# Three passes instead of triples: the order of the split products in a chunk, and where TensorE waits for the low weights

## The chip, the core and the metric

The kernel runs on one core of a Trainium2 chip. Its engines work side by side and meet through semaphores: TensorE (PE) multiplies, VectorE (DVE), ScalarE (ACT) and GpSimd (POOL) do the elementwise work, SyncE (SP) issues loads. The metric is the device time in microseconds of one execution; the median over several executions counts.

## What is computed

The reference is one inference step of a decoder trunk of two layers, for 256 prompt positions and 8 sampled ones (264 token columns in all), with a model width of 2048. Cut to what matters here:

```python
def _layer(x, ...):
    xn = _rms_norm(x, g_pre_mix)
    proj = xn @ w_in                       # 2048 x 6144 columns here
    ...                                    # retention, mLSTM and pooling heads on proj
    mixed = concatenate([ret_out, mlstm_out, pool_out]) @ w_out
    x = x + _rms_norm(mixed, g_post_mix)
    hn = _rms_norm(x, g_pre_ffn)
    ff = (silu(hn @ w_ffn_gate) * (hn @ w_ffn_up)) @ w_ffn_down
    x = x + _rms_norm(ff, g_post_ffn)
```

All of it is in fp32. The outputs are the updated x for prompt and samples and the new states of the heads, for both layers. Nearly all arithmetic lies in the four matrix products with `w_in`, `w_out`, gate and up, and down.

## The kernel before, in words

Activations lie transposed, with 128 features on the partitions and the 264 tokens as columns. A weight matrix comes in **chunks**: a chunk is 128 x 2048 words and holds sixteen 128 x 128 blocks of weights, all that one output tile of 128 features needs (for the down projection a chunk has eleven blocks, and an output tile takes two chunks). A layer has 216 chunks, numbered in the order of their use: 0 to 47 for `w_in`, 48 to 63 for `w_out`, 64 to 107 gate and up of the first half of the hidden units, 108 to 139 down for it, 140 to 183 and 184 to 215 the same for the second half.

An fp32 product is done as three products in a faster rounded format (fp32r). Each operand is split into a rounded high part and a low part, the rest. A block's product is then high weights x high operand, high weights x low operand, low weights x high operand, all added up in one PSUM bank. These are lines 463, 464 and 465, three matrix products of 128 x 128 weights by 264 columns for each block, 48 in a chunk.

A chunk passes through four engines:
- SP loads it into one of four slots of `raw` (line 395) when the chunk four before it has been used.
- ACT copies it, rounded, into one of two slots of `whi` (line 741, the high part), when it has landed and the chunk two before it has been used. It counts `hi_made`.
- DVE subtracts high from raw and writes the low part `wlo` over the raw slot (line 1010). It counts `chunk_split`.
- TensorE waits for a free PSUM bank (`tile_evac`) and for `chunk_split`, does the 48 products, and counts `chunk_used`.

DVE then takes the result out of the bank. In the projections of `w_in` it multiplies it by the reciprocal norm (lines 1278 to 1291); the four banks 0 to 3 are used in turn.

The order of the work on each engine is written out by hand. Between the chunks of `w_in` a table, `SCHEDULE`, puts steps of the heads on every engine: TensorE does chunk n and then its part of the steps listed for n, DVE and ACT their parts of the same steps and their part of the split for chunk n + 2. For n from 15 to 41 DVE does the steps first and the low part of chunk n + 2 behind them (line 1300). Retention head h has its scores behind chunk 29 + 2h (`ret_scores`, L618), its states behind chunk 30 + 2h (`ret_states`, L626 and L630) and its outputs behind chunk 31 + 2h (`ret_outputs`, L640 to L645). The outputs wait for DVE's lines 1197 and 1203 (`ret_s2`, `ret_snew`).

Two kinds of chunks are special. The first chunk after a norm (0 and 64, `fresh`) has the sums of squares for the norm between its products (`square_sum`, L439) and waits for each block of its operand. Chunk 48, the first of `w_out`, does the block of the last retention head at its end and waits for it there (`last_ready`); its start also waits for the pooling heads (`pl_lo`).

Of the kernel before, what the change touches and what calls it, by code (L numbers as in the profile page):

```python
# [23 lines left out]
P = 128  # L24
# [3 lines left out]
KT = D_MODEL // P  # L28
# [162 lines left out]
def build(nc, a, gamma, gchunk):  # L191
    with ExitStack() as ctx:
# [3 lines left out]
        start = base0 - 212800  # L196

        def place(name, shape, dt, at=None):

            n = 4  # L200
            for s in shape[1:]:
                n *= s
            if at is None:
                at = used[0]
                used[0] += (n + 31) // 32 * 32
                assert used[0] <= 212800, (name, used[0])
            t = nc.alloc_sbuf_tensor_at(name, shape, dt, offset=start + at)
            return t, at
# [11 lines left out]
        wlo, _ = place("wlo", [P, RAW, CHUNK], F32R, at_raw)  # L220
# [69 lines left out]
        late = proj[:, T_MO:NPROJ, :].rearrange("p a t -> p (a t)")  # L290
# [18 lines left out]
        def cnt(name, unit=1, head=0):  # L309
            c = Count(sem(name), unit, head)  # L310
            if head:
                ahead.append(c)
            return c
# [5 lines left out]
        hi_made = cnt("hi_made")  # L319
        chunk_split = cnt("chunk_split")  # L320
# [101 lines left out]
        def _(pe):  # L422
            pe.wait_ge(*dve_done(3))
            with pe.Fori(0, DEPTH) as l:
# [11 lines left out]
                def square_sum(m, k):  # L436

                    pe.wait_ge(*sqx_made(l * 2 * KT + m * KT + k + 1))
                    pe.matmul(bank[4][:, 0:TOK], ones, sq[:, k % 4, :], start=k == 0, stop=k == KT - 1)\  # L439
                        .then_inc(*sqx_used.up)  # L440

                def chunk(n, slot, hi_slot, out, operand, ks, start, stop, fresh=None, last_ready=None):

                    if fresh:
                        e, m, lead = fresh
                        pe.wait_ge(*rms_made(l * 4 + e))
                        for k in range(lead):
                            square_sum(m, k)  # L450
                    pe.wait_ge(*chunk_split(n + 1))
                    high = whi_spare if hi_slot is None else whi[:, hi_slot]
                    for k, tile in enumerate(ks):
                        w = bass.ds((tile - min(ks)) * P, P)
                        hi, lo = operand(tile)
                        first, last = start and k == 0, stop and k == len(ks) - 1
                        if last and last_ready:
                            pe.wait_ge(*last_ready)
                        if fresh:
                            if k + lead < KT:  # L460
                                square_sum(m, k + lead)
                            pe.wait_ge(*operand_lo(l * 2 * KT + m * KT + k + 1))
                        pe.matmul(out, high[:, w], hi, start=first, stop=False)  # L463
                        pe.matmul(out, high[:, w], lo, start=False, stop=False)  # L464
                        mm = pe.matmul(out, wlo[:, slot, w], hi, start=False, stop=last)  # L465
                    mm.then_inc(*chunk_used.up)


# [9 lines left out]
                def whole_tile(c, o, j, operand, fresh=None, hi_slot=0):  # L478

                    pe.wait_ge(*tile_evac(o - BANKS + 1))  # L480
                    chunk(c, j, hi_slot, bank[j][:, 0:TOK], operand, range(KT), True, True, fresh)
# [207 lines left out]
                for j in range(RAW):  # L689
                    c, o_ = l * N_CHUNKS + C_OUT + j, l * N_TILES + O_OUT + j  # L690
                    if j == 0:

                        pe.wait_ge(*tile_evac(o_ - BANKS + 1))
                        pe.wait_ge(*mixed_ready(2 * l + 1))
                        pe.wait_ge(*pl_lo(l + 1))
                        chunk(c, j, 0, bank[j][:, 0:TOK], of_mixers, [k for k in range(KT) if k != RH - 1] + [RH - 1],
                              True, True, last_ready=mixed_ready(2 * l + 2))
                    else:
                        whole_tile(c, o_, j, of_mixers, hi_slot=j % HI)
                whole(1, KT // RAW, C_OUT, O_OUT, of_mixers)  # L700
                acc_sum(1)
                for b in range(NBLK):
                    if b == 0:
                        for j in range(RAW):
                            whole_tile(l * N_CHUNKS + C_GU[0] + j, l * N_TILES + O_GU[0] + j, j, of_x,
                                       (2, 1, 2) if j == 0 else None, FIRST_GU[j])
                    whole(1 if b == 0 else 0, 2 * BT // RAW, C_GU[b], O_GU[b], of_x)
                    with pe.Fori(0, KT // 4) as i:
                        for j in range(8):
                            u, half = j // 2, j % 2  # L710
                            if j < 2:
                                pe.wait_ge(*hidden_ready(l * FT + b * BT + (half + 1) * HT))
                            if half == 0:
                                pe.wait_ge(*tile_evac(l * N_TILES + O_DN[b] + i * 4 + u - BANKS + 1))
                            chunk(l * N_CHUNKS + C_DN[b] + i * 8 + j, j % RAW, j % HI, bank[u][:, 0:TOK], of_hidden,
                                  range(half * HT, (half + 1) * HT), half == 0, half == 1)
# [926 lines left out]
```

## Time and profile before

| | |
|---|---|
| median of 3 runs | 2576.87 us (2573.36 to 2578.7) |
| the profiled execution | 2579.15 us |
| its span (first to last instruction) | 2577.5 us |
| PE busy | 2496.9 us, 97% |
| PE weight loads busy | 2454.4 us, 95% |
| DVE busy | 1438.3 us, 56% |
| ACT busy | 1060.9 us, 41% |
| POOL busy | 301.8 us, 12% |
| mean granted TensorE clock | 0.984 of full |
| chain of work that ended last | PE 90% of it; L463, L464 and L465 28% each |

Busy times are those of one execution. Matrix products are pipelined: each is shown for about 0.28 us, but one starts about every 0.12 us, so a busy share near 100% says that the stream does not break, and how fast it runs is read from start to start. An engine's idle time matters only where the next engine waits for it. The view of who waited for whom takes an idle time from the modelled end of the instruction before.

### The profile page before, as it was taken

What the parts mean: (1) busy time and instruction counts of PE and PEld (TensorE: products, weight loads), DVE (VectorE), ACT (ScalarE), POOL (GpSimd) and SP (SyncE); (2) the same over time, 40 slices, a digit from 0 to 9 for tenths busy, and PEclk for the clock granted to TensorE, in tenths of its full rate; (3) what the DMA queues carried; (4) which work ended last, traced back from release to release, by engine and by line L of the source; (5) the groups of instructions that cost most, each with busy time, mean ns of one, the idle gap of its engine ahead of it and who ended that gap; (6) DMA issues with size and microseconds to landing.
All of it is one profiled execution on the core that took longest, in us unless ns stands there. A gap on an engine that the chain in (4) does not pass through costs nothing.

```text
span 2577.5 us, 50784 instructions
## 1 busy us (share of the span) xinstructions
PE 2496.9 (97%) x20192; PEld 2454.4 (95%) x20192; DVE 1438.3 (56%) x1669; ACT 1060.9 (41%) x1298; POOL 301.8 (12%) x264
## 2 busy tenths in 40 slices
PE   8999999899999999999899999998999999999996
PEld 7999999899999999999799999898999999999996
DVE  5577564755554455554575774647555544555445
ACT  5433554444433343333344345534443333343432
POOL 1001143400000000002310012343000000000023
PEclk9999999999999999999899999999999999999998
DMA  6444644355545555545444455443555455555453
GB/s 256 166 164 141 209 158 171 123 180 179 180 164 181 195 182 184 183 162 181 167 161 172 150 163 190 148 176 118 181 180 182 166 179 194 184 182 181 158 182 118
DMA packets 70613, 443.86 MB, mean 172 GB/s; under 512 B 8512, under 2 KB 8736, under 8 KB 31456
## 3 DMA queue, kind: packets, MB, share of 16 engines
q1 hardware_dynamic: 62784, 413.23, 45.9%
q0 software_dynamic: 6992, 26.82, 3.3%
q10 hardware_dynamic: 720, 2.24, 0.2%
q8 instruction: 74, 1.21, 0.2%
q14 instruction: 43, 0.35, 0.0%
HBM read 427.10 MB, written 15.16 MB: 172 GB/s over the span
## 4 chain that ended last, share of the span: by engine, by line
PE 90%; DVE 3%; issue 3%; ACT 2%; POOL 1%; DMA 1%; DVEq 0%; ACTq 0%; POOLq 0%; SPq 0%
PE bank L463 28%; PE bank L464 28%; PE bank L465 28%; DVE wlo L1010 1%; ACT whi L741 1%; PE bank L574 1%; PE bank L645 1%; POOL x L1421 1%; PE bank L439 1%; PE bank L492 1%; DMA pool_p<-proj 0%; DVE alo L1016 0%; DVE work L1027 0%; PE bank L529 0%; ACT v_spread L851 0%
## 5 line engine op out<-in xcount | busy, mean ns | idle before, releaser
L463 PE MATMUL bank<-ahi,whi 128*128 128x264 f32 x4288 | 1231.4, 287 | 8.4 <-DVE wlo L1010 6.8
L465 PE MATMUL bank<-ahi,wlo 128*128 128x264 f32 x4352 | 1236.1, 284 | 0.0
L464 PE MATMUL bank<-alo,whi 128*128 128x264 f32 x4288 | 1218.8, 284 | 0.0
L741 ACT ACTIVATE whi<-raw 128x2048 fp32r<-128x2048 f32 (+1 forms) x428 | 751.7, 1756 | 1124.6 <-PE bank L465 1117.1
L1010 DVE TENSOR_TENSOR wlo<-raw,whi 128x2048 fp32r<-128x2048 f32 (+1 forms) x428 | 897.5, 2097 | 561.3 <-ACT whi L741 561.1
L463 PEld LDWEIGHTS bank<-ahi,whi 128*128 128x128 f32 x4288 | 811.7, 189 | 17.4 <-DVE wlo L1010 9.4
L465 PEld LDWEIGHTS bank<-ahi,wlo 128*128 128x128 f32 x4352 | 820.4, 189 | 0.0
L464 PEld LDWEIGHTS bank<-alo,whi 128*128 128x128 f32 x4288 | 812.2, 189 | 1.7
L463 PE MATMUL bank<-hhi,whi 128*128 128x264 f32 x1408 | 401.0, 285 | 1.9 <-DVE hlo L1354 1.9
L465 PE MATMUL bank<-hhi,wlo 128*128 128x264 f32 x1408 | 399.9, 284 | 0.0
L464 PE MATMUL bank<-hlo,whi 128*128 128x264 f32 x1408 | 397.4, 282 | 0.0
L463 PEld LDWEIGHTS bank<-hhi,whi 128*128 128x128 f32 x1408 | 265.0, 188 | 2.7 <-issue 2.7
L464 PEld LDWEIGHTS bank<-hlo,whi 128*128 128x128 f32 x1408 | 265.1, 188 | 0.0
L465 PEld LDWEIGHTS bank<-hhi,wlo 128*128 128x128 f32 x1408 | 264.9, 188 | 0.0
L1404 POOL TENSOR_TENSOR ssq<-sq,zero 128x264 f32<-128x264 f32 x4 | 8.5, 2127 | 1314.2 <-ACT sq L746 1314.2
L463 PE MATMUL bank<-mixed,whi 128*128 128x264 f32 x512 | 146.1, 285 | 5.0 <-DVE mixed L1032 5.0
L1404 POOL TENSOR_TENSOR ssq<-sq,ssq 128x264 f32<-128x264 f32 x56 | 115.7, 2067 | 267.5 <-ACT sq L746 267.5
L465 PE MATMUL bank<-mixed,wlo 128*128 128x264 f32 x512 | 146.2, 286 | 0.0
L464 PE MATMUL bank<-mixed,whi 128*128 128x264 f32 x512 | 146.1, 285 | 0.0
L963 ACT ACTIVATE hhi<-work 128x264 f32 (+1 forms) x88 | 37.4, 425 | 242.8 <-DVE work L1351 242.8
L1346 DVE TENSOR_TENSOR work<-bank,rstd 128x264 f32<-128x264 f32 x88 | 38.0, 432 | 142.0 <-PE bank L465 142.0
L463 PEld LDWEIGHTS bank<-mixed,whi 128*128 128x128 f32 x512 | 97.1, 190 | 5.4 <-issue 5.4
(239 smaller groups left out, 1718.4 us busy)
## 6 DMA issues: line engine op xcount, KB each, us to landing
raw<-w_gu SPq DMA_DIRECT2D x176, 1024.0 KB, 4.7
raw<-w_in SPq DMA_DIRECT2D x96, 1024.0 KB, 4.8
raw<-w_dn SPq DMA_DIRECT2D x128, 704.0 KB, 4.1
raw<-w_out SPq DMA_DIRECT2D x32, 1024.0 KB, 4.8
work<-s_ret POOLq DMA_DIRECT2D x12, 512.0 KB, 4.6
ret_s<-work POOLq DMA_DIRECT2D x12, 512.0 KB, 3.3
proj<-s_c POOLq DMA_DIRECT2D x8, 576.0 KB, 4.6
c_s<-proj POOLq DMA_DIRECT2D x8, 576.0 KB, 4.0
```

The costliest lines, as they stand in the source:

```text
L439: pe.matmul(bank[4][:, 0:TOK], ones, sq[:, k % 4, :], start=k == 0, stop=k == KT - 1)\
L463: pe.matmul(out, high[:, w], hi, start=first, stop=False)
L464: pe.matmul(out, high[:, w], lo, start=False, stop=False)
L465: mm = pe.matmul(out, wlo[:, slot, w], hi, start=False, stop=last)
L492: return pe.matmul(out, in_, ident[0:n, 0:n], is_transpose=True, start=True, stop=True)
L574: pe.matmul(bank[bk][rows, SEQ + b:SEQ + b + 1], Cs[0:MQK, b, f0:f1], qt[:, SEQ + b:SEQ + b + 1], start=True, stop=True)
L645: mm = pe.matmul(bank[7][:, SEQ + b:SEQ + b + 1], S[:, h % 2, b, :], q[:, SEQ + b:SEQ + b + 1], start=True, stop=True)
L741: act.activation(high[:, 0:words], raw[:, slot, 0:words], ACT.Copy).then_inc(*hi_made.up)
L963: act.activation(hhi[:, i * 2 + u, :], hs[:, u, :], ACT.Copy).then_inc(*hidden_hi.up)
L1010: dve.tensor_tensor(wlo[:, slot, w], raw[:, slot, w], high[:, w].bitcast(F32), ALU.subtract)\
L1346: dve.tensor_tensor(ua[:, u, :], bank[j][:, 0:TOK], rstd[:], ALU.mult).then_inc(*tile_evac.up)
L1404: pool.tensor_tensor(ssq[:], sq[:, slot, :], zero[:] if first else ssq[:], ALU.add).then_inc(*sq_added.up)
```

## The change

It touches only TensorE's function `chunk`. In an ordinary chunk the sixteen products of high weights with the high operand come first, then the sixteen of high weights with the low operand, then the sixteen of low weights with the high operand. The wait at the start is for the high weights (`hi_made`); the wait for the low weights (`chunk_split`) stands ahead of the third pass. Chunks 0 and 64 keep their triples and both waits at the start. Chunk 48 does fifteen blocks in passes and the last block as a triple, with its wait, at the end. The number of products, weight loads and bytes is the same.

```diff
--- before.py
+++ after.py
@@ -448,21 +448,37 @@
                         pe.wait_ge(*rms_made(l * 4 + e))
                         for k in range(lead):
                             square_sum(m, k)
-                    pe.wait_ge(*chunk_split(n + 1))
                     high = whi_spare if hi_slot is None else whi[:, hi_slot]
-                    for k, tile in enumerate(ks):
-                        w = bass.ds((tile - min(ks)) * P, P)
-                        hi, lo = operand(tile)
-                        first, last = start and k == 0, stop and k == len(ks) - 1
-                        if last and last_ready:
-                            pe.wait_ge(*last_ready)
-                        if fresh:
+                    low = wlo[:, slot]
+                    pe.wait_ge(*hi_made(n + 1))
+                    if fresh:
+                        pe.wait_ge(*chunk_split(n + 1))
+                        for k in ks:
+                            w = slice(k * P, (k + 1) * P)
+                            hi, lo = operand(k)
                             if k + lead < KT:
                                 square_sum(m, k + lead)
                             pe.wait_ge(*operand_lo(l * 2 * KT + m * KT + k + 1))
-                        pe.matmul(out, high[:, w], hi, start=first, stop=False)
-                        pe.matmul(out, high[:, w], lo, start=False, stop=False)
-                        mm = pe.matmul(out, wlo[:, slot, w], hi, start=False, stop=last)
+                            pe.matmul(out, high[:, w], hi, start=k == 0, stop=False)
+                            pe.matmul(out, high[:, w], lo, start=False, stop=False)
+                            mm = pe.matmul(out, low[:, w], hi, start=False, stop=k == KT - 1)
+                    else:
+                        late = [ks[-1]] if last_ready else []
+                        early = ks[:-1] if last_ready else ks
+                        for part, (weights, of) in enumerate(((high, 0), (high, 1), (low, 0))):
+                            if part == 2:
+                                pe.wait_ge(*chunk_split(n + 1))
+                            for k, tile in enumerate(early):
+                                w = bass.ds((tile - min(ks)) * P, P)
+                                mm = pe.matmul(out, weights[:, w], operand(tile)[of], start=start and part == 0 and k == 0,
+                                               stop=stop and not late and part == 2 and k == len(ks) - 1)
+                        for tile in late:
+                            w = bass.ds((tile - min(ks)) * P, P)
+                            hi, lo = operand(tile)
+                            pe.wait_ge(*last_ready)
+                            pe.matmul(out, high[:, w], hi, start=False, stop=False)
+                            pe.matmul(out, high[:, w], lo, start=False, stop=False)
+                            mm = pe.matmul(out, low[:, w], hi, start=False, stop=True)
                     mm.then_inc(*chunk_used.up)
 
 
```

TensorE, first layer's head steps, from the states of a retention head to the next chunk (`v_spread` and `vk_rows` are operands of the states, `ahi` and `alo` the parts of the normed x, `whi` and `wlo` the parts of the weights). Before:

```order
L630 MATMUL bank<-v_spread,vk_rows 128x512 [waits ret_diag]
L630 MATMUL bank<-v_spread,vk_rows 128x512
L480 REGISTER_ALU
L451 REGISTER_ALU [waits tile_evac]
L463 MATMUL bank<-ahi,whi 128x264 [waits chunk_split]
L464 MATMUL bank<-alo,whi 128x264
L465 MATMUL bank<-ahi,wlo 128x264
L463 MATMUL bank<-ahi,whi 128x264
```

and now:

```order
L646 MATMUL bank<-v_spread,vk_rows 128x512 [waits ret_diag]
L646 MATMUL bank<-v_spread,vk_rows 128x512
L496 REGISTER_ALU
L453 REGISTER_ALU [waits tile_evac]
L473 MATMUL bank<-ahi,whi 128x264 [waits hi_made]
L473 MATMUL bank<-ahi,whi 128x264 x15
L473 MATMUL bank<-alo,whi 128x264 x16
L473 MATMUL bank<-ahi,wlo 128x264 [waits chunk_split]
L473 MATMUL bank<-ahi,wlo 128x264 x15
```

The wait for `chunk_split` stood on the first of the 48 products and now stands on the 33rd, and the first waits for `hi_made`; the alternation of three is gone.

TensorE, the end of chunk 48 and the start of the next (`mixed` holds both parts of the mixers' output). Before:

```order
L465 MATMUL bank<-mixed,wlo 128x264
L463 MATMUL bank<-mixed,whi 128x264 [waits mixed_ready]
L464 MATMUL bank<-mixed,whi 128x264
L465 MATMUL bank<-mixed,wlo 128x264
L480 REGISTER_ALU
L451 REGISTER_ALU [waits tile_evac]
L463 MATMUL bank<-mixed,whi 128x264 [waits chunk_split]
```

and now the whole chunk 48, and the register step behind it:

```order
L473 MATMUL bank<-mixed,whi 128x264 [waits hi_made]
L473 MATMUL bank<-mixed,whi 128x264 x29
L473 MATMUL bank<-mixed,wlo 128x264 [waits chunk_split]
L473 MATMUL bank<-mixed,wlo 128x264 x14
L479 MATMUL bank<-mixed,whi 128x264 [waits mixed_ready]
L480 MATMUL bank<-mixed,whi 128x264
L481 MATMUL bank<-mixed,wlo 128x264
L496 REGISTER_ALU
```

The wait for the last block's operand, `mixed_ready`, stands on the 46th product in both, and the wait on `pl_lo` ahead of the chunk's first; only `chunk_split` moved.

## Rows read from the trace of the kernel before

**Rows 1.** costliest groups: line, engine, operands, count | busy us, mean ns | idle before.

```profile
L463 PE MATMUL bank<-ahi,whi 128*128 128x264 f32 x4288 | 1231.4, 287 | 8.4 <-DVE wlo L1010 6.8 <-DVE alo L1016 1.5
...
L463 PE MATMUL bank<-hhi,whi 128*128 128x264 f32 x1408 | 401.0, 285 | 1.9 <-DVE hlo L1354 1.9
...
L463 PE MATMUL bank<-mixed,whi 128*128 128x264 f32 x512 | 146.1, 285 | 5.0 <-DVE mixed L1032 5.0
...
L463 PE MATMUL bank<-ahi,whi_spare 128*128 128x264 f32 x64 | 24.7, 386 | 0.0
```

**Rows 2.** busy time by stretches, TensorE alone: stretch, length, busy (count), clock, DMA.

```profile
399.00:469.00 70.00, 70.00 (x579) 1.00 0.52 181
520.00:750.00 230.00, 230.00 (x1905) 1.00 0.50 177
800.00:870.00 70.00, 70.00 (x581) 1.00 0.53 177
```

**Rows 3.** timeline of the second gate and up block: start, length, instruction, idle before.

```profile
1000.84 2.29 DVE L1010 TENSOR_TENSOR wlo<-raw,whi 128x2048 fp32r<-128x2048 f32 x1 [1.43 <-ACT whi L741]
...
1004.37 0.28 PE L465 MATMUL bank<-ahi,wlo 128*128 128x264 f32 x1
1004.49 0.28 PE L463 MATMUL bank<-ahi,whi 128*128 128x264 f32 x1
```

**Rows 4.** who waited for whom on TensorE: us in total, times, longest us.

```profile
PE bank L463 <- DVE wlo L1010: 6.8, 8, 2.6
```

**Rows 5.** timeline of TensorE, first layer, before chunk 39.

```profile
318.75 0.71 PE L630 MATMUL bank<-v_spread,vk_rows 72*128 72x512 f32 x2
320.70 0.39 PE L463 MATMUL bank<-ahi,whi 128*128 128x264 f32 x1 [1.24 <-DVE wlo L1010]
```

**Rows 6.** timeline of TensorE, first layer, before chunk 33.

```profile
270.71 0.71 PE L630 MATMUL bank<-v_spread,vk_rows 72*128 72x512 f32 x2
271.26 0.28 PE L463 MATMUL bank<-ahi,whi 128*128 128x264 f32 x1
```

**Rows 7.** timeline of TensorE, first layer, before chunk 41.

```profile
336.29 0.71 PE L630 MATMUL bank<-v_spread,vk_rows 72*128 72x512 f32 x2
337.95 0.39 PE L463 MATMUL bank<-ahi,whi 128*128 128x264 f32 x1 [0.95 <-DVE wlo L1010]
```

**Rows 8.** timeline of TensorE, before chunk 30 and before chunk 32.

```profile
247.64 0.61 PE L618 MATMUL bank<-proj 128*128 128x128 f32 x4
248.44 0.39 PE L463 MATMUL bank<-ahi,whi 128*128 128x264 f32 x1 [0.19 <-DVE wlo L1010]
...
264.11 0.61 PE L618 MATMUL bank<-proj 128*128 128x128 f32 x4
264.48 0.37 PE L463 MATMUL bank<-ahi,whi 128*128 128x264 f32 x1
```

**Rows 9.** timeline of TensorE, from down projection to the next block.

```profile
887.77 0.28 PE L465 MATMUL bank<-hhi,wlo 128*128 128x264 f32 x1
888.38 0.39 PE L463 MATMUL bank<-ahi,whi 128*128 128x264 f32 x1 [0.33 <-DVE wlo L1010]
```

**Rows 10.** timeline of TensorE, second layer, before chunk 39.

```profile
1596.30 0.71 PE L630 MATMUL bank<-v_spread,vk_rows 72*128 72x512 f32 x2
1599.65 0.40 PE L463 MATMUL bank<-ahi,whi 128*128 128x264 f32 x1 [2.64 <-DVE wlo L1010]
```

**Rows 11.** timeline of VectorE, first layer, during chunk 39.

```profile
322.01 1.28 DVE L1203 SCALAR_TENSOR_TENSOR work<-work,bank 128x512 f32<-128x512 f32 x2
...
323.56 2.28 DVE L1010 TENSOR_TENSOR wlo<-raw,whi 128x2048 fp32r<-128x2048 f32 x1
```

**Rows 12.** timeline of VectorE and TensorE, first layer, during and behind chunk 41.

```profile
341.19 1.28 DVE L1203 SCALAR_TENSOR_TENSOR work<-work,bank 128x512 f32<-128x512 f32 x2
...
344.53 1.84 PE L645 MATMUL bank<-proj,work 128*128 128x1 f32 x16
```

**Rows 13.** busy time by stretches, TensorE alone, around the gap of rows 10.

```profile
1599.00:1604.00 5.00, 4.35 (x23) 0.66 0.34 136
```

## The prediction, made before the changed kernel ran

> **What bounds the kernel now.** I read the page first, then the waits of TensorE, then the timeline at each place where those waits stand, and last the busy time by stretches. In the costliest groups the reader is to see that three lines, L463, L464 and L465, are nearly all of TensorE's work: 4288 + 64 (the group of `whi_spare`) + 1408 + 512 = 6272 products each, 18,816 together [rows 1]. In a stretch without waits they start one behind the other: 230 us hold 1905 of them [rows 2]; less the two or so that run over the edges that is 0.121 us each, and 18,816 × 0.121 = 2277 us of the span's 2577.5. So the time is TensorE's stream of products plus the gaps in it. DVE and ACT are busy 56% and 41% of the span and are ahead of TensorE nearly everywhere. The steady case: the low part of a chunk is done at 1000.84 + 2.29 = 1003.13 us, and the chunk that needs it begins at 1004.49, 1.36 us later [rows 3]. There the wait that is moved costs nothing now, and can give nothing.
>
> What is left for it is one row of the waits: L463 stood 6.8 us for DVE's L1010 in 8 places [rows 4]. The idle times of 5.0 us before the `mixed` products and of 1.9 us before the `hhi` products end with other waits, which stay ahead of the products [rows 1].
>
> **The change part by part.**
> *The wait on the low weights goes from the first product to the 33rd.* I price each of the 8 places by what starts when, since an idle time is counted from a modelled end. The four in the first layer:
> - Chunk 39: from the first L630 to the first L463 it is 320.70 − 318.75 = 1.95 us [rows 5]; at an undisturbed place of the same form 271.26 − 270.71 = 0.55 us [rows 6]. Gain 1.40 us.
> - Chunk 41: 337.95 − 336.29 = 1.66, less 0.55: 1.11 us [rows 7].
> - Chunk 30: from L618 to L463 0.80 us, undisturbed 0.37: 0.43 us [rows 8].
> - The first chunk of the second gate and up block: 888.38 − 887.77 = 0.61, where two products otherwise stand 0.12 apart: 0.49 us [rows 9].
> That is 3.43 us. The second layer repeats three of them within 0.01 us, and at its chunk 39 the gap is 1599.65 − 1596.30 = 3.35 us, so 2.80 us come free [rows 10]; together 4.83 us. Both layers: 8.3 us.
>
> *Is the wait late again at its new place?* The third pass starts 32 × 0.121 = 3.9 us behind the chunk's start (22 products, 2.7 us, in the down projection). The chunk that gains most starts 2.80 us earlier, so its low part comes 1.1 us before it is wanted. In the steady chunks it is there before the first product. ACT's high part, which the first product now waits for, ends before the low part begins everywhere, since DVE subtracts it.
>
> *What is late next?* Behind chunk 39 TensorE does the retention outputs, which need DVE's L1203, and then chunk 40, which needs DVE's next L1010. In the first layer these end at 322.01 + 1.28 = 323.3 and 323.56 + 2.28 = 325.8 us [rows 11]; TensorE would finish chunk 39 at 320.70 − 1.40 + 5.8 = 325.1, and chunk 40 begins more than 3 us behind that. Neither holds it. Behind chunk 41 the L1203 ends at 341.19 + 1.28 = 342.47, and L645, which waits for it, starts at 344.53 [rows 12]. L645 would come 1.40 + 1.11 = 2.51 us earlier, at 342.02; L1203 hangs on TensorE's steps behind chunk 39 and moves by 1.40, to 341.07. That leaves 1.0 us: the gain eats most of the slack, but is not given back. The waits farther on (`mixed`, `hlo`, and the norms between sublayers) start from the end of a TensorE chunk and so keep their length. If L1203 did not move at all, 342.47 − 342.02 = 0.45 us a layer would be lost, 0.9 us in all.
>
> *The wait itself.* There are as many products, weight loads and bytes as before. Each chunk has one more wait and register step, in the middle of a stream. At a chunk's start two such waits and a register step stand today, and the last product of one chunk and the first of the next still start 0.12 us apart [rows 3]; TensorE's queue covers them, and I price the new one at nothing. The upper bound is a product that restarts the stream: it lasts 0.39 us instead of 0.28 [rows 5, 6], 0.11 × 432 chunks = 48 us, if every one of the new waits broke the stream. The row of the chunk's start is the nearer one, so this end gets no more than the slower stream below has. Nor is there a gain in it: nothing is taken out of the stream.
>
> *The clock.* TensorE's clock fell behind the 2.8 us gap of the second layer: the 5 us around it have a mean granted clock of 0.66, so the lower level of 1.2 GHz for most of them, and hold 23 products in 4.35 busy us, where 36 would fit at 2.4 GHz: 13 × 0.121 = 1.6 us [rows 13]. Without the gap this is not due. But such a fall need not stand in every run, and another gap may get one instead; I take nothing for it and keep ±1.6 us.
>
> *The order of the products.* Before, the two products of a tile share their weights, and the first and third their moving operand. Afterwards neighbours share neither: each takes the next 128 × 128 of weights and the next 264 columns. Rows can only bound what this does to the spacing. Three orders of operands are in the trace: x in 230 us 1905, the mixers' output in 70 us 579, the hidden units in 70 us 581 [rows 2]. With 2.3 taken off for the edges (each runs 0.28 us) that is 120.9, 121.4 and 121.0 ns. The spacing so does move with the operands, by some 0.5 ns, which over 18,816 products is ±9 us. I take zero, since no row leans to a side, and ±0.35 ns, ±6.6 us, as the usual size.
>
> The Trainium skill has a rule for this spacing (TensorE: Matmul & The Clock Gate, "Back-to-back issue gap"): at the high clock it is the column count over 2.4 GHz plus about 2.5 ns. For 264 columns that gives 112.5 ns, an estimate by that page; the trace does not agree, with 120.9 [rows 2]. In it the order of operands plays no part; by the rule the sum is 2568.6 with nothing around it, by the three rows it is 2568.6 ± 9.
>
> **The sum.** Against the profiled execution: 2579.15 − 8.3 = 2570.9 us (2569.3 with the clock). Its span is 2577.5 and 1.65 us lie around it, which stay. That execution was 2.3 us over the median of the runs, 2576.87, so for the median I forecast 2576.87 − 8.3 = 2568.6 us.
>
> **The rivals.**
> - *The gain is given back.* TensorE comes earlier to joins at which DVE, ACT and POOL are no earlier; DVE's chain behind chunk 39 is dense, and the slack that shrinks from 2.1 to 1.0 us behind chunk 41 speaks for it. Against it: most later waits are counted from TensorE's own end. If the four retention gaps (1.40 + 1.11 + 2.80 + 1.11 = 6.4 us) came back as waits, 1.9 us would be left: 2575.0 us. 15%.
> - *A slower stream.* The place is every chunk: the new sequence of operand reads spaces products wider. It decides from 8.3 / 18,816 = 0.44 ns on, and is told apart from no change from (8.3 + 5.2) / 18,816 = 0.72 ns. At 1.0 ns: 2568.6 + 18.8 = 2587.4 us. For it: spacing depends on operands, and a neighbour's shared weights or columns might help today. Against: orders as different as x and mixed stand 0.5 ns apart. 12%.
> - *A quicker stream.* The same at −0.6 ns: 2568.6 − 11.3 = 2557.3 us. 13%.
> - *The wait does not move in effect,* since TensorE's sequencer would stop at the later wait just as long. It would need low parts later than 3.9 us behind the start, and no row has one; 2576.9 us. 2%.
>
> **How the numbers follow.** The forecast has 58%. About 0.2%, 5.2 us, is what a measurement of this kernel can tell from no change. The forecast with its ±6.6 us for order and ±1.6 for the clock reaches over that line in part (8.3 − 5.2 = 3.1 us), the first rival stands on the side of no change, the third on that of faster. I give two thirds of the forecast to faster. Summed: faster 0.60, same 0.28, slower 0.12. The range reaches from the quicker stream at 2557 to just over the time before, 2579.
>
> **What would show it.** In the changed kernel's waits the row of L463 for `wlo` should be gone, and no row of the third pass for `wlo` should stand in its place; from L630 to the next chunk's first product it should be 0.55 us everywhere. The waits for `mixed` and `hlo` should be 5.0 and 1.9 us as before. 230 us of the gate and up stage should hold 1905 products: 1894 (0.7 ns more each) would mean the slower stream, 1914 the quicker one. The forecast is wrong if the count differs by more than these, if ret_snew becomes a wait at the retention outputs, or if the first spacing at the 33rd product is over 0.13 us.

## The result, and the profile after

The changed kernel takes 2571.07 us (median of 20 executions, 2561.91 to 2577.77) against 2576.8 us (20 executions, 2569.33 to 2580.9, and one of 6630.32 us). The ratio is 0.9972, interval 0.9962 to 0.9982: faster by 0.28%, 7.2 us; the two medians are 5.7 us apart. Forecast were 2568.6 us and 8.3 us less. The profiled execution takes 2573.19 us, its span is 2571.6 us against 2577.5, at a mean granted clock of 0.983 against 0.984.

The waits of TensorE after the change, in total us, times, longest; the two rows of products that are left:

```profile
PE bank L473 <- DVE mixed L1048: 5.0, 2, 2.5
...
PE bank L473 <- DVE hlo L1370: 1.9, 4, 0.5
```

The row for `wlo`, 6.8 us in 8 places [rows 4], is gone, and the third pass has none. The waits for `mixed` and `hlo` are what they were, 5.0 and 1.9 us [rows 1]. The timeline of TensorE around chunk 39 of the first layer (answers to [rows 5]), the start of its third pass, and VectorE's low part for it:

```profile
319.87 0.61 PE L642 MATMUL bank<-work 128*128 128x128 f32 x4
320.23 0.71 PE L646 MATMUL bank<-v_spread,vk_rows 72*128 72x512 f32 x2
320.77 2.00 PE L473 MATMUL bank<-ahi,whi 128*128 128x264 f32 x15
```

```profile
324.69 0.76 PE L473 MATMUL bank<-ahi,wlo 128*128 128x264 f32 x5
```

```profile
319.44 2.70 DVE L1026 TENSOR_TENSOR wlo<-raw,whi 128x2048 fp32r<-128x2048 f32 x1
```

From L646 to the first product it is 320.77 − 320.23 = 0.54 us, as at the undisturbed place [rows 6], instead of 1.95. The low part ends at 319.44 + 2.70 = 322.14, 1.4 us behind the chunk's start; the third pass begins at 324.69, 2.5 us later. In the second layer the gap is 0.54 us too, instead of 3.35 [rows 10], and the third pass begins 2.8 us behind the low part's end.

Behind chunk 41 the join that I had watched [rows 12], VectorE and then TensorE:

```profile
341.21 1.28 DVE L1219 SCALAR_TENSOR_TENSOR work<-work,bank 128x512 f32<-128x512 f32 x2
```

```profile
343.33 1.84 PE L661 MATMUL bank<-proj,work 128*128 128x1 f32 x16
```

L1219 (1203 before) ends at 342.49 and the products that need it start at 343.33: 0.84 us to spare, where 1.0 was forecast and 2.1 stood before.

The spacing, from busy time by stretches (answers to [rows 2]: 579, 1905, 581 products there):

```profile
399.00:469.00 70.00, 70.00 (x577) 1.00 0.50 180
520.00:750.00 230.00, 230.00 (x1906) 1.00 0.50 178
800.00:870.00 70.00, 70.00 (x583) 1.00 0.54 178
```

Counted start to start over whole chunks, the spacing in x is 120.83 ns before and after, to the last digit: a chunk of 48 takes 5.800 us in both orders. In the down projection it falls from 121.11 to 120.71 ns (4224 products, −1.7 us), in the output projection it rises from 121.39 to 121.67 (1536, +0.4 us).

What took some of the gain away shows in the same view over the head steps: stretch, length, busy (count), granted clock. Before, then after:

```profile
94.00:235.00 141.00, 141.00 (x1110) 0.96 0.47 156
235.00:385.00 150.00, 146.52 (x1210) 1.00 0.52 176
...
1370.00:1510.00 140.00, 140.00 (x1108) 0.96 0.46 153
1510.00:1660.00 150.00, 145.11 (x1180) 0.99 0.51 175
```

```profile
94.00:235.00 141.00, 141.00 (x1090) 0.94 0.45 150
235.00:385.00 150.00, 148.89 (x1230) 1.00 0.53 182
...
1370.00:1510.00 140.00, 140.00 (x1085) 0.94 0.46 153
1510.00:1660.00 150.00, 148.89 (x1224) 1.00 0.51 175
```

In the stretches 235 to 385 and 1510 to 1660, where the gaps were, TensorE now does 20 and 44 products more. In 94 to 235 and 1370 to 1510, the mLSTM heads, it does 20 and 23 fewer, 20 × 0.121 = 2.4 and 2.8 us: the mean clock there is 0.94 instead of 0.96. The changed code adds no wait there. Counted over whole chunks, 15 to 28 of the two layers, the loss is 6.2 us. Nine products with high weights at the lower level of the clock, and sixteen with the low operand at the full one, in the changed kernel:

```profile
139.05 2.33 PE L473 MATMUL bank<-ahi,whi 128*128 128x264 f32 x9
```

```profile
316.01 2.09 PE L473 MATMUL bank<-alo,whi 128*128 128x264 f32 x16
```

Nine products take 2.33 us in the one, sixteen take 2.09 us in the other. The first stretch is chunk 18, behind the mLSTM outputs, whose 32 products have one column each, where an ordinary product has 264.

The whole difference of the two profiled spans, worked out from chunk to chunk: gaps −8.4 us, clock behind the gap of the second layer's chunk 39 −1.6, spacing −1.4, clock in the mLSTM heads (chunks 15 to 28) +6.2, all the rest −0.7; together −5.9, which is 2571.6 − 2577.5.

### The profile page after: what moved, and what is told of

Its sections match the earlier page's. It is cut to its first block, busy times and chain, and to the rows that moved or that the text cites. A ratio compares the mean times of both kernels' runs of the same rounds, so it can differ in the third digit from the quotient of the medians.

```text
span 2571.6 us, 50788 instructions
## 1 busy us (share of the span) xinstructions
PE 2498.7 (97%) x20192; PEld 2458.4 (96%) x20192; DVE 1437.0 (56%) x1669; ACT 1061.3 (41%) x1298; POOL 301.9 (12%) x264
## 4 chain that ended last, share of the span: by engine, by line
PE 93%; issue 2%; DVE 2%; ACT 1%; POOL 1%; DMA 0%; DVEq 0%; ACTq 0%; POOLq 0%; SPq 0%
PE bank L473 85%; PE bank L590 1%; ACT whi L757 1%; PE bank L661 1%; PE bank L439 1%; DVE wlo L1026 1%; PE bank L508 1%; POOL x L1437 1%; DVE work L1043 0%; DVE alo L1032 0%; PE bank L545 0%; DMA raw<-w_in 0%; PE bank L571 0%; PE bank L563 0%; PE bank L646 0%
## 5 line engine op out<-in xcount | busy, mean ns | idle before, releaser
L473 PE MATMUL bank<-ahi,whi 128*128 128x264 f32 x4256 | 571.7, 288 | 0.0
L473 PE MATMUL bank<-ahi,wlo 128*128 128x264 f32 x4288 | 561.3, 284 | 0.0
L473 PE MATMUL bank<-alo,whi 128*128 128x264 f32 x4256 | 559.1, 284 | 0.0
L473 PEld LDWEIGHTS bank<-ahi,whi 128*128 128x128 f32 x4256 | 542.3, 191 | 5.9 <-issue 3.8
L473 PEld LDWEIGHTS bank<-ahi,wlo 128*128 128x128 f32 x4288 | 535.6, 188 | 0.0
L473 PEld LDWEIGHTS bank<-alo,whi 128*128 128x128 f32 x4256 | 533.8, 189 | 0.0
L473 PE MATMUL bank<-hhi,whi 128*128 128x264 f32 x1408 | 191.1, 284 | 1.9 <-DVE hlo L1370 1.9
L473 PE MATMUL bank<-hhi,wlo 128*128 128x264 f32 x1408 | 191.7, 284 | 0.0
L473 PE MATMUL bank<-hlo,whi 128*128 128x264 f32 x1408 | 190.1, 283 | 0.0
L473 PE MATMUL bank<-mixed,whi 128*128 128x264 f32 x1020 | 130.7, 286 | 5.0 <-DVE mixed L1048 5.0
```

Source lines behind the costliest of these rows:

```text
L473: mm = pe.matmul(out, weights[:, w], operand(tile)[of], start=start and part == 0 and k == 0, stop=stop and not late and part == 2 and k = ...
```

## The experiments

Each is timed against the kernel before in its own series, and there were four series: a ratio can be carried from one to another, a difference of medians only within some 4 us, since the kernel before itself has medians from 2573.18 to 2576.8. "At 0.988" is the median of those executions of a kernel whose mean granted clock was 0.988.

| kernel | median us (n) | lowest to highest | ratio, interval | at 0.988 |
|---|---|---|---|---|
| before, beside the changed one | 2576.8 (20) | 2569.33 to 2580.9, one of 6630.32 | | |
| before, beside e1 to e4 | 2575.46 (31) | 2565.54 to 2584.2 | | 2571.6 (9) |
| before, beside e5 | 2576.66 (17) | 2567.33 to 2585.62 | | |
| before, beside e12 | 2573.18 (8) | 2569.35 to 2582.15 | | |
| changed | 2571.07 (20) | 2561.91 to 2577.77 | 0.9972, 0.9962 to 0.9982 | 2562.6 (4) |
| e1 order only | 2571.38 (12) | 2567.89 to 2577.66 | 0.9988, 0.9975 to 1.0001 | 2569.3 (6) |
| e2 four chunks a layer | 2565.08 (12) | 2561.72 to 2573.87 | 0.9966, 0.9952 to 0.9981 | 2563.1 (5) |
| e3 pairs | 2579.63 (12) | 2576.8 to 2588.05 | 1.003, 1.0014 to 1.0045 | 2578.6 (5) |
| e4 outputs in two pieces | 2564.00 (8) | 2562.64 to 2564.86 | 0.9958, 0.9943 to 0.9972 | all at 0.989 |
| e5 the same on before | 2575.52 (12) | 2570.29 to 2581.34 | 0.9994, 0.9979 to 1.0009 | 2575.1 (9) |
| e12 e4, one more wait moved | 2560.69 (5) | 2558.95 to 2562.42 | 0.9947, 0.9928 to 0.9966 | nearly all at 0.989 |

**e1_order_only.** The changed kernel with the low weights waited for at the start.

```diff
-                            if part == 2:
+                            if part == 0:
                                 pe.wait_ge(*chunk_split(n + 1))
```

> The changed kernel with one line moved: the wait for the low weights stands at the chunk's first product again, the products stay in three passes. Theory A (the moved wait is the gain): the eight gaps before L473 come back, 6.8 us by the view of waits; what is left is what the order of the products does to the spacing, in the two traces 121.11 to 120.71 ns in the down projection (4224 products, -1.7 us) and 121.39 to 121.67 ns in the output projection (1536 products, +0.4 us), so 1.3 us under the kernel before, about 2575.5 us, ratio 0.9995. Theory B (the order of the products itself is the gain): the time stays at that of the changed kernel, about 2571 us, ratio 0.997.

TensorE's waits in it:

```profile
PE bank L473 <- DVE mixed L1048: 5.2, 2, 2.6
PE bank L473 <- ACT whi L757: 3.2, 3, 1.1
...
PE bank L473 <- DVE wlo L1026: 2.8, 5, 1.3
PE bank L473 <- DVE hlo L1370: 2.4, 4, 0.6
```

The waits are back: 3.2 + 2.8 = 6.0 us in 8 places (some now put down to ACT's `whi`, since the first product waits for both). The median alone, 2571.38, would have spoken for theory B, but half the executions, the profiled one among them, had a mean clock of 0.988. Its ratio, 0.9988 (0.9975 to 1.0001), takes in theory A's 0.9995 and leaves out B's 0.997, though its interval overlaps that of the changed kernel. At 0.988 it stands 6.7 us over the changed kernel and 2.3 us under the one before. With the waits back in their places, theory A holds; the order alone gives the 1.3 us of the spacing and perhaps one more. The restarts show something else: with two waits in a row ahead of a product, each late start is 0.11 to 0.13 us later than before (ahead of chunk 30 0.57 us instead of 0.46, chunk 140 0.74 instead of 0.61).

**e2_four_chunks.** Passes only in chunks 30, 39, 41 and 140 of each layer, the triples elsewhere.

```diff
+                    elif not passes:
+                        pe.wait_ge(*chunk_split(n + 1))
...
                     else:
                         late = [ks[-1]] if last_ready else []
...
-                               n % HI)
+                               n % HI, n in (30, 39, 41))
```

> Triples and the wait at the start as in the kernel before, except in chunks 30, 39, 41 and 140 of each layer, which are done in three passes with the wait ahead of the third. Theory A: all eight waits for the low weights go with these eight of 432 chunks; the spacing in the down projection stays 121.1 ns; so about 8 us under the kernel before, 2568 to 2571 us, ratio 0.997. Theory B: eight chunks' order is nothing, the time stays at 2576 us, ratio 1.000.

```profile
PE bank L439 <- ACT sq L790: 31.0, 22, 11.1
PE bank L439 <- DVE wlo L1042: 8.4, 1, 8.4
PE bank L473 <- DVE mixed L1064: 5.2, 2, 2.6
PE bank L433 <- ACT sq L778: 3.0, 4, 0.9
PE bank L473 <- DVE hlo L1386: 2.3, 4, 0.6
PE bank L695 <- DVE proj L1252: 2.2, 2, 1.1
```

No row for `wlo` before a tile's product is left (the second row is the norm at the start, as ever), and the time is that of the changed kernel: ratio 0.9966 against 0.9972, with intervals that overlap. Eight of 432 chunks carry the whole gain. The median, 2565.08 us, lies under the 2568 to 2571 forecast and 6 us under the changed kernel's; most of that goes with the clock, for at 0.988 the two are 0.5 us apart.

**e3_pairs.** The first two passes woven together, the third as in the changed kernel.

```diff
+                        for k, tile in enumerate(early):
...
+                            mm = pe.matmul(out, high[:, w], hi, start=start and k == 0, stop=False)
+                            mm = pe.matmul(out, high[:, w], lo, start=False, stop=False)
+                        pe.wait_ge(*chunk_split(n + 1))
...
```

> The changed kernel with the first two passes woven together: for each block the high weights with the high and then with the low operand, so neighbours share their weights as in the kernel before, and the low weights as a last pass behind their wait. Theory A: no wait for the low weights, as in the changed kernel, ratio 0.997. Theory C (the spacing follows the sequence of operand addresses, not the sharing of weights): the spacing in the stretches of x stays 120.8 ns, since both parts of x lie alike, and in the down and output projections lies between 120.7 and 121.7 ns. Rival D (shared weights make a product dearer or cheaper): the spacing moves the same way in all three, by 0.3 ns or more; 0.3 ns is 5.6 us.

Busy time by stretches, x and down projection:

```profile
520.00:750.00 230.00, 230.00 (x1891) 1.00 0.50 179
800.00:870.00 70.00, 70.00 (x578) 1.00 0.53 182
```

1891 products where 1906 were: 121.81 ns in x, 121.62 in the down projection. Theory A's ratio of 0.997 and theory C's 120.8 ns in x both missed; a rise in all three against the kernel before is what rival D had forecast. The waits are gone as in the changed kernel, and the kernel is still slower than before by 0.3%: 12,864 ordinary products of x × 0.97 ns + 4224 × 0.91 ns + 0.2 = 16.5 us, against 16.0 us at 0.988. So a slower stream from the order alone, my rival, is real; this order has it and the changed one doesn't. The next five, single executions, ask what makes it.

**e7_zigzag, e8_reverse, e9_alike, e10_stride3, e11_stride5.** The changed kernel with another sequence inside the passes: e7, e8, e9, and e10 (e11 has 5 for 3).

```diff
+                                if part < 2:
+                                    of = (part + k) % 2
```

```diff
-                            for k, tile in enumerate(early):
+                            for k, tile in enumerate(list(early)[::-1] if not late else early):
```

```diff
-                            for k, tile in enumerate(early):
+                            for k, tile in enumerate(early if late else [early[q] for q in (sorted(range(len(early)), key=lambda q: (q % 8, q)))]):
```

```diff
-                            for k, tile in enumerate(early):
+                            for k, tile in enumerate(early if late else [early[q] for q in [3 * q % len(early) for q in range(len(early))]]):
```

> The changed kernel with the operand alternating inside the first two passes: the first pass takes the high operand for even and the low one for odd blocks, the second the other way round; no two neighbours share weights. In e3_pairs, where neighbours shared weights and the operand alternated too, the spacing in x was 121.8 ns, against 120.83 in the changed kernel. Theory H (shared weights of neighbours made e3_pairs slower): 120.8 ns in x here. Theory I (the alternation between the two operand arrays did): 121.8 ns or nearly.

> The changed kernel with the blocks of each pass taken from the last to the first (chunk 48 excepted). Nothing else changes: as many products, no shared neighbours, each pass through one operand array. Theory C (the spacing depends on the sequence of addresses, not on what is shared): it leaves 120.83 ns in x and 120.71 ns in the down projection, by 0.2 ns or more in one of them. Rival J (it depends only on whether neighbours share something): it stays within 0.05 ns in both.

> The changed kernel with the blocks of each pass in the order 0, 8, 1, 9, 2, 10 and so on (chunk 48 excepted). The sixteen blocks' operands start at 1056-byte steps, so blocks k and k + 8 start alike in 256 bytes: neighbours of a pass now lie alike in pairs, as the high and low operand of one block did in e3_pairs, but share no weights. Theory C (the spacing follows the sequence of operand addresses): in x it comes to e3_pairs' value for its woven part, 122.3 ns, in all three passes. Theory H (shared weights made e3_pairs slower): it stays at 120.8 ns.

> The changed kernel with the blocks of each pass in steps of three (0, 3, 6, and so on, modulo their number; chunk 48 excepted). Theory C: the spacing in x differs from both 120.83 ns (upwards) and 121.67 ns (downwards, e8_reverse); it may be lower, and the bound of what could be had is the 116 ns that single products show, 18,000 x 4.8 ns = 87 us. If nothing lies under 120.8 ns, the order of the changed kernel is as good as any of the five tried.

> As e10_stride3, in steps of five. Theory C: again a value of its own in x, between 120 and 123 ns.

Spacing in ns, start to start over whole chunks of x, of the down and of the output projection. The last column is the time of the single execution, beside 2576.66 us (median of 17) of the kernel before for e7 and e8 and a single 2580.92 us for e9 to e11:

| sequence | x | down | output | us |
|---|---|---|---|---|
| triples (before) | 120.83 | 121.11 | 121.39 | |
| passes (changed) | 120.83 | 120.71 | 121.67 | |
| e3 pairs | 121.81 | 121.62 | 121.81 | |
| e7 zigzag | 120.83 | 121.31 | 122.08 | 2566.48 |
| e8 reverse | 121.67 | 122.12 | 122.09 | 2587.82 |
| e9 alike | 122.29 | 121.31 | 121.81 in the first layer, 122.64 in the second | 2587.71 |
| e10 steps of 3 | 120.83 | 121.62 | 121.60 | 2565.87 |
| e11 steps of 5 | 122.29 | 122.32 | 121.81 | 2594.54 |

The stretch of x in e7, e8 and e9:

```profile
520.00:750.00 230.00, 230.00 (x1905) 1.00 0.51 179
```

```profile
520.00:750.00 230.00, 230.00 (x1893) 1.00 0.51 178
```

```profile
520.00:750.00 230.00, 230.00 (x1883) 1.00 0.51 178
```

e9 decides: its neighbours share no weights, but their operands start alike in 256 bytes, as in e3's woven part. Its spacings within a chunk begin 121, 126, 123, 123, 122, 121, 121, 116 ns, those of e3's 121, 126, 123, 124, 121, 121, 121, 116. Theory H falls, and theory C holds in its main point: the spacing moves with the sequence of the operands' addresses, whether or not weights are shared. e7 by itself had come out as H forecast, 120.83 ns in x; it threw out theory I only. It agrees with C as well: the high and low part of x lie alike in 256 bytes, so swapping them changes nothing in x, while in the other two, where not all do, it costs 0.4 to 0.6 ns. Rival J fell with e8. But C did not foresee the values: e10 was to leave 120.83 ns in x and stayed on it, and e11 was to have a value of its own and has that of e9, though its neighbours don't lie alike. And the sequence isn't the whole cause: in e9's output projection the two layers run the same sequence from the same addresses, the one at 121.81 ns, the other at 122.64. Why a sequence is slower stays open; no sequence was under 120.83 ns in x.

**e4_spread.** The changed kernel, and the mLSTM outputs of a head in two pieces: the second bank's products and the sums go behind the first pass of the next chunk.

```diff
+                            if part == 1 and between:
+                                between()
...
-                    for bk, (f0, f1), po in ((4, big, 0), (5, small, 64 * odd)):
+                    for bk, (f0, f1), po in ((4, big, 0), (5, small, 64 * odd))[piece:piece + 1]:
```

> The changed kernel with the mLSTM outputs cut in two on TensorE: the sixteen-fold products into the first bank stay behind chunk 17, 20, 23 and 26, those into the second bank and the row sums go behind the first pass of the next chunk. Theory E (the executions differ by how often TensorE's clock falls at these products of one column): no stretch at the lower clock starts between 94 and 235 us or in the same place of the second layer, the mean granted clock is 0.988 or more, the times scatter by under 6 us, the median is 2560 to 2564 us, ratio 0.994. Rival F (the mLSTM chain is what TensorE waits for): the sums come 1.9 us later, VectorE's reciprocal norm ends later than chunk 18, TensorE waits for it at the next head's scores, 6 times some 1 us, and the time is that of the changed kernel or more.

```profile
94.00:235.00 141.00, 139.66 (x1134) 1.00 0.48 159
...
1370.00:1510.00 140.00, 138.67 (x1125) 1.00 0.46 154
```

The clock is 1.00 in both mLSTM stretches, with 1134 and 1125 products instead of 1090 and 1085. The eight executions, all with a mean clock of 0.989, lie within 2.2 us, where those of the changed kernel lie within 16. Theory E holds. Rival F has a small part, though not at the scores: TensorE now waits 1.3 us twice for an ACT step of the mLSTM norm. So most of the scatter of the changed kernel was how often its clock fell there; where it fell is seen in the profiled execution only, for the others the mean clock speaks.

**e5_before_spread.** The same two pieces in the kernel before.

```diff
                     for k, tile in enumerate(ks):
+                        if k == 5 and between:
+                            between()
```

> The kernel before with the mLSTM outputs cut in two on TensorE as in e4_spread; the second piece stands behind the fifteenth product of the next chunk. Beside e4_spread this shows the change without the scatter of the clock. Theory A: the difference is the eight gaps, 8.3 us, and the spacing of the down and output projections, 1.3 us: 9.6 us over e4_spread's 2564.0, so 2573.6 us, with a scatter of under 3 us and a mean clock of 0.989. Rival (part of the gain of the change, 5.7 us between the medians, is in the clock, or the gaps are partly given back): the difference is 6 us or less, 2570 us.

The wait for the low weights in it, and VectorE's wait for the store of the pool state at the pooling head's finish, in e5 and in the kernel before (first and second layer of each):

```profile
PE bank L465 <- DVE wlo L1020: 9.3, 8, 3.3
```

```profile
312.30 0.17 DVE L1256 SCALAR_TENSOR_TENSOR proj<-work,proj 128x8 f32<-128x8 f32 x1 [5.54 <-DMA pool_p<-proj]
...
1591.72 0.17 DVE L1256 SCALAR_TENSOR_TENSOR proj<-work,proj 128x8 f32<-128x8 f32 x1 [4.74 <-DMA pool_p<-proj]
```

```profile
312.76 0.17 DVE L1246 SCALAR_TENSOR_TENSOR proj<-work,proj 128x8 f32<-128x8 f32 x1 [2.98 <-DMA pool_p<-proj]
...
1591.71 0.17 DVE L1246 SCALAR_TENSOR_TENSOR proj<-work,proj 128x8 f32<-128x8 f32 x1 [4.38 <-DMA pool_p<-proj]
```

The scatter was forecast under 3 us and is 11 us, with mean clocks from 0.986 to 0.990. 2575.5 over 2564.0 is 11.5 us, against theory A's 9.6; through the ratios to the kernel before, 0.9994 and 0.9958, it is 9.3 us, nearer to theory A than to the rival's 6 us or less, though the two intervals leave some 5 us either way. The waits are 9.3 us here instead of 6.8 [rows 4]. VectorE stands for a transfer of 30 KB, `pool_p`, for 5.54 and 4.74 us instead of 2.98 and 4.38, so its low part for chunk 39 comes later, and TensorE's gap there is 3.67 and 3.39 us instead of 1.64 and 3.04. With those gaps theory A gives 9.6 + 2.4 = 12.0 us for this execution. And the clock takes its part: it is 1.00 in both mLSTM stretches, but it falls behind the gaps ahead of chunk 39. The stretch of the first layer:

```profile
235.00:385.00 150.00, 144.21 (x1166) 0.98 0.50 169
```

Chunk 39 takes 2.8 us longer here than in e4 in the first layer and 1.6 us in the second. The changed kernel has neither the gaps nor, in the traces at hand, these falls; that they make up the scatter that is left is likely, but only one execution shows where it fell.

**e6_more_waits.** Three more satisfied waits in each chunk.

```diff
+                                if k == 8:
+                                    pe.wait_ge(*hi_made(n + 1))
```

> The changed kernel with a further wait, on the already counted high part, ahead of the ninth product of each of the three passes: 3 more waits in each of 427 chunks, all of them satisfied. Theory A (a satisfied wait in the stream is covered by TensorE's queue): the spacing stays at 120.83 ns in the stretches of x and 120.71 ns in the down projection, and the span changes by under 1 us beside the clock. Rival G (each such wait costs the 0.11 us by which the restarts behind a second wait grew in e1_order_only): 3 x 427 x 0.11 = 141 us, spacing 127.7 ns.

```profile
520.00:750.00 230.00, 230.00 (x1905) 1.00 0.51 180
800.00:870.00 70.00, 70.00 (x583) 1.00 0.54 181
```

Busy time by stretches: 1905 and 583 products against 1906 and 583 without them, and 120.833 ns; the single execution takes 2572.46 us. A satisfied wait inside a running stream costs nothing; rival G is out. The 0.11 us of e1 are paid only when the stream restarts.

**e12_hidden_late.** e4, and the last hidden block of the second in every eight down chunks (109, 117 and so on) as a triple at the end; only at chunks 109 and 185 is its wait one that TensorE had stood for.

```diff
-                                pe.wait_ge(*hidden_ready(l * FT + b * BT + (half + 1) * HT))
+                                pe.wait_ge(*hidden_ready(l * FT + b * BT + (half + 1) * HT - half))
...
+                                  last_ready=hidden_ready(l * FT + b * BT + BT) if j == 1 else None)
```

> e4_spread, and in the second chunk of each group of down chunks the last hidden block is done as a triple at the end with its wait there, as the changed kernel does with the last retention head. The chunk's start then waits for one hidden block less. If the waits of this kernel come free in the way those for the low weights did, the four gaps of 0.77 us ahead of chunks 109 and 185 shrink to 0.12 us, 2.6 us under e4_spread, 2561.4 us, ratio 0.994, scatter under 3 us. Rival: the order of the operands in that chunk (one of eight down chunks) spaces its products wider, or the last block's wait shows at its new place, and nothing is left of it.

```profile
PE bank L475 <- DVE mixed L1059: 5.0, 2, 2.5
PE bank L433 <- ACT sq L773: 3.0, 4, 0.9
PE bank L611 <- ACT proj L854: 2.7, 2, 1.3
PE bank L684 <- DVE proj L1247: 2.2, 2, 1.1
...
PE bank L666 <- DVE work L1230: 0.3, 1, 0.3
```

The row for `hlo`, 1.9 us, is gone, the four gaps are 0.12 us instead of 0.77, 2.6 us together. The median is 3.3 us under e4's, but from another series; by the ratios, 0.9947 and 0.9958, the two are 2.8 us apart, with intervals that overlap. At 2560.69 us it has the lowest median here. The last row is the join behind chunk 41: TensorE stands 0.3 us for L1230, the `ret_snew` step, there, and it does so in e6 too.

## Why the prediction was right

- *The eight gaps, 8.3 us.* Right in each place: every gap went to the undisturbed spacing, and e2 shows that nothing else is needed. As a size the term rested on one execution: the two gaps ahead of chunk 39 are set by a store and vary, 1.6 to 3.7 us and 1.4 to 3.4 us over the traces, so the term runs from about 7 to 11 us.
- *Not late again, no new wait.* Right: 2.5 and 2.8 us to spare at the third pass of the two chunks 39. With the longest gap seen, 3.67 us (e5), it would be some 0.4 us. At the join behind chunk 41 0.84 us are left for 1.0. In the traces of e6 and e12 this join has become a wait of 0.3 us, once in each; of the rival "given back" there is that much, and no more.
- *The new wait at nothing.* Right (e6).
- *The order of the products, 0 ± 6.6 us.* In size right, −1.3 us by the spacings. The bound was too narrow: I took 0.5 ns from three rows, and the tried orders span 1.5 ns in x, 27 us if they reached all products. The sums of before and after agree in x exactly, which no row told me; a pass in steps of five would have made the change slower than before.
- *The rule of the Trainium skill* (TensorE: Matmul & The Clock Gate, "Back-to-back issue gap"). The formula that I took from it, 112.5 ns for 264 columns, is by that section the gap of a single product issued alone. For a stream of weight loads and products the section says that both set the spacing, and gives about 81 ns at 128 columns and about 131 ns at 512; the 120.7 to 122.6 ns here lie between. It has no place for the order, and eight orders with one column count gave eight sets of spacings, so here the measurement decides against it as a complete rule.
- *The clock, ± 1.6 us.* This is the mis-sized term. I looked only at the fall behind the gap. The falls behind the mLSTM outputs cost 6.2 us more in the profiled execution, and between executions up to 14 us: 2562.6 at 0.988, 2577 at 0.982. e4 removes them and leaves 2564.0. So that the median came within 2.5 us of the forecast is in part luck. With equal clocks the change is worth 9.0 us (2571.6 against 2562.6) instead of the 7.2 measured over all; the runs at 0.988 of the two come from different series, so this is a comparison of medians, not an interval.
- *The chances.* They don't follow from their parts: the first rival's 2575.0 us is 1.9 us from the time before and so belongs to "same". Two thirds of 58% and the 13% of the quicker stream make 0.52 for faster, where 0.60 was given, and the rest makes 0.36 for same instead of 0.28.

Whether the changed order makes falls of the clock more frequent was not settled. The changed kernel had 7 of its 20 executions at a mean clock of 0.983 or less, the kernel before 4 of 56 in the three series that list it, although it has the falls behind chunk 39 on top; but e1, with the same order, had none of 12, and 6 of them at 0.988, where the changed kernel had 4 of 20. If it does, a part of what the gaps gave is lost again by the change itself.

## What to carry to other kernels

A wait belongs at the first instruction that needs its data, and an order of work that puts all users of the late operand last makes room for it; but only the few places where the wait is seen to end an idle time pay, and doing it there alone (e2) was as good here. When products are reordered for it, the spacing of a long unbroken stretch is to be compared before and after, since the sequence of operand addresses can cost more than the waits give. And a scatter of executions that is wider than the effect should be looked up in the granted clock of each before medians are compared.

## What the runs showed of the hardware

- The spacing of 264-column products moves with the sequence of operand start addresses. In the changed kernel, with a step of 1056 bytes, it repeats every eight blocks within a nanosecond (8 × 1056 is a multiple of 256). Over the orders tried it ranges from 120.83 to 122.29 ns in x. One sequence can have two values: 121.81 and 122.64 ns in e9's output projection.
- A satisfied wait inside the stream is free (e6, one execution, three more in each of 428 chunks); two waits in a row at a restart cost 0.11 to 0.13 us more than one (e1).
- Two times sixteen products of one column with a few others between (L590), 4 us in which TensorE counts as busy, are followed by stretches at 1.2 GHz in the profiled executions of both kernels, though not behind every head. Cut in two by fifteen or sixteen wide products they are followed by none in the profiled executions of e4, e5 and e12.
